# One table set for the roots, low weights a word past a line, constants behind the second piece

## The chip, the cores and the metric

The kernel runs on one core of one Trainium2 chip, as one program. The metric is the device time of an execution in microseconds, the median over several. A profiled execution adds the trace that the rows below are from; its span runs from the first to the last instruction.

## The reference

Two stages over 256 tokens of width 2048, all in fp32, and a final normalization. `first_block` has two layers, the first with an RWKV7 and RG-LRU mixer, the second with an attention over selected keys; `second_block` has two layers of three attentions side by side. What matters here:

```python
def rms_norm(x, g, eps=1e-6):
    xf = x.astype(jnp.float32)
    return (xf * lax.rsqrt(jnp.mean(xf * xf, -1, keepdims=True) + eps) * g).astype(x.dtype)

def layer_norm(x, g, b, eps=LN_EPS):
    ...
    return ((xf - mu) * lax.rsqrt(var + eps) * g + b).astype(x.dtype)

for layer in range(DEPTH):            # first_block
    y = ... @ w_out                   # the mixer, itself products of x
    x = layer_norm(DN_ALPHA * x + y, ...)
    x = layer_norm(DN_ALPHA * x + conv_ffn(x, ffn_w_up, ..., ffn_w_down), ...)
    x = x + sigmoid(x @ ple_w_gate) * (p @ ple_w_proj)
```

Nearly all of the work is products of the 2048 x 256 activations with weight matrices that are read once from memory.

## The kernel before

Activations are kept transposed, features on the 128 partitions and the 256 tokens in the free dimension, so a tensor of 2048 features is 16 tiles of 256 columns. A weight matrix comes in pieces of 128 x 4096 words (16 input tiles by 256 output features, 2,048 KB), which the SP queue brings into a ring of three slots (`load` and `stream`, L671 and L692). The second product of the feed-forward block has pieces of 11 input tiles (1,408 KB).

A product of fp32 numbers is made of three products of rounded ones (fp32r). ACT copies one half of a piece (128 output features, 128 x 2048 words) with rounding into the high weights `WHI` (`split`, L1771), and DVE subtracts these from the piece and writes the low weights `WLO` (`split`, by the helper at L2506). The activations have a high and a low part as well, side by side (`pair`). For each half, `wide_half` on PE runs 16 matmuls of the high weights on the 512 columns of both parts (L863), then 16 of the low weights on the 256 columns of the high part (L849). The feed-forward block's second product does the same with 11 and 11 (L968 and L973, weights `DHI` and `DLO`). A matmul is two instructions, a load of 128 columns of weights and the pass of the activations. PE waits on `w_hi` ahead of the high run and on `w_lo` ahead of the low one.

`spl_r` is a part of one big arena and holds high 0, low 0, high 1, low 1, each of 2048 words without a gap; `dsp_r` likewise with 1408 words each. All of them begin on a multiple of 32 bytes. `LG` and `BF` are other uses of the same words at other times.

An inverse root, 1/sqrt(v), is made on ACT as exp(-0.5 ln v). There are 16 places: the four layer norms in `normed` (L1896 and L1898), the norm of the keys in the first mixer (L2097 and L2099), two in `inverse_root` (L2235 and L2237), three in `rms` (L2332 and L2334), two `mn` (L2357 to L2360) and four `dn` (L2454 and L2456) in `second_block`. ACT holds one set of function tables at a time. The compiler puts an ACT_TABLE_LOAD right ahead of an ACTIVATE whose function the current set hasn't, and it takes one set for Ln and another for Exp, where one set would hold both. The Tanh of `second_block` (L2391) has no load of its own in the trace.

SP's queue begins with quarters of x and of the first piece ea0 in turn (`first_quarters`), then the second piece ea1, then `constants` (vec 789.5 KB, mat 896 KB, relb 2 KB, posi 129 KB; L654 to L657), then the third piece ea2, and from there each piece waits for its slot. DVE's first use of vec is the small set-up operation that writes `omm`.

Of the kernel before, what the change touches and what calls it, by code (L numbers as in the profile page):

```python
# [14 lines left out]
T = 256  # L15
P = 128
D = 2048
DT = D // P
# [6 lines left out]
SPL = 19456  # L25
# [2 lines left out]
MB = 5  # L28
FC = 11
HHW = FT * T  # L30
SCR = 2 * (HHW + FC * 2 * P) - 2 * T
PI_BELOW = 3.1415925
BIG_NEG = -1e30
NOT_ALLOWED = -3.0e38
# [190 lines left out]
def build(nc, dram, out):  # L225
# [38 lines left out]
    with ctx:  # L264
# [20 lines left out]
        FR = mybir.dt.float32r  # L285
        arena = nc.sbuf_base + (-nc.sbuf_base) % 32
        sb("arena", 2 * DT * T + SCR + 2 * T)
        X = DT * T

        def named(name, at_, width, dt=F):  # L290
            return nc.alloc_sbuf_tensor_at(name, [P, width], dt, offset=arena + 4 * at_)

        xa, xb, scr = named("xa", 0, X), named("xb", X, X), named("scr", 2 * X, SCR)
        xa_r, xb_r = named("xa_r", 0, X, FR), named("xb_r", X, X, FR)
        scr_r, spl_r = named("scr_r", 2 * X, 2 * HHW, FR), named("spl_r", 2 * X + SPL, 8192, FR)

        dsp_r = named("dsp_r", 2 * X + 2 * HHW, 4 * FC * P, FR)

        rstd = named("rstd", 2 * X + SCR, 2 * T)
        all_r = named("all_r", 0, 2 * X + SCR, FR)  # L300
        scrv = scr_r[:, :].rearrange("p (a t) -> p a t", t=T)
        allv = all_r[:, :].rearrange("p (a t) -> p a t", t=T)
        xav = xa[:, :].rearrange("p (a t) -> p a t", t=T)
# [6 lines left out]
        def v(name, i=0, n=1):  # L310
            return vec[:, VCOL[name] + i:VCOL[name] + i + n]
# [23 lines left out]
        S = {n: ctx.enter_context(nc.semaphore(n)) for n in names}  # L335
        x_part = [ctx.enter_context(nc.semaphore(f"x_part{i}")) for i in range(4)]
        w_part = [ctx.enter_context(nc.semaphore(f"w_part{i}")) for i in range(3)]
        w_ready = [ctx.enter_context(nc.semaphore(f"w_ready{i}")) for i in range(R3)]
# [19 lines left out]
        def job_free(j):  # L358
            return mb_free[j % MB]
# [47 lines left out]
        SE = sumbuf[:, 0:3 * T].rearrange("p (b t) -> p b t", t=T)  # L407
        KNB = sumbuf[:, 3 * T:5 * T]
        GNB = [sumbuf[:, (3 + n) * T:(4 + n) * T] for n in range(2)]
        LG = scr[:, SPL + 4096:SPL + 6144].rearrange("p (k n) -> p k n", n=P)  # L410
        VTOK = scr[:, 13056:15104].rearrange("p (t c) -> p t c", t=2)
        YT = tiles(15104, 16)
        XC = xbv[:, 0:8]
        KZ = xbv[:, 8:16]
        AR = xb[:, :].rearrange("p (a t x n) -> p a t x n", a=8, t=2, x=2)
        BF = [scr[:, SPL + 4096 * t:SPL + 4096 * t + 2048].rearrange("p (u x) -> p u x", u=16) for t in range(2)]
        GVB = [xtra[:, 1024 * t:1024 * (t + 1)].rearrange("p (u x) -> p u x", u=16) for t in range(2)]
        KF = [ring[:, SLOT + 512 * g:SLOT + 512 * (g + 1)].rearrange("p (u x) -> p u x", u=4) for g in range(4)]
        MN = [ring[:, SLOT + 512 * g:SLOT + 512 * (g + 1)].rearrange("p (u x n) -> p u x n", u=4, x=2) for g in range(4)]
# [76 lines left out]
        def squares(k):  # L496
# [11 lines left out]
        ANG = scr[:, 11776:12544]  # L508


        WHI, WLO = ([spl_r[:, 4096 * h + o:4096 * h + o + 2048].rearrange("p (k n) -> p k n", n=P)
                     for h in range(2)] for o in (0, 2048))

        DHI, DLO = ([dsp_r[:, FC * P * (2 * h + o):FC * P * (2 * h + o + 1)].rearrange("p (k n) -> p k n", n=P)
                     for h in range(2)] for o in range(2))
        HLO = scr_r[:, 0:HHW].rearrange("p (a t) -> p a t", t=T)


# [125 lines left out]
        def _(sp):  # L644
# [6 lines left out]
                        .then_inc(w_part[q] if q < 3 else w_ready[0], 16)  # L651

            def constants():
                sp.dma_start(vec[:, :], dram["vec"]).then_inc(S["in_vec"], 16)  # L654
                sp.dma_start(mat[:, :], dram["mat"]).then_inc(S["in_mat"], 16)
                sp.dma_start(relb[0:32, :], dram["relb"]).then_inc(S["in_mat"], 16)
                sp.dma_start(posi[:, :], dram["posi"]).then_inc(S["in_mat"], 16)  # L657
# [46 lines left out]
            load("ev_out", 0)  # L704

            sp.wait_ge(S["g_done"], STEP0["ev_out"] - 2)
            sp.dma_start(scr[:, SPL + 4096:SPL + 6144], dram["lg"][0]).then_inc(S["in_lg"], 16)

            sp.wait_ge(S["elem"], 3)
            for part in range(X_PARTS):  # L710
# [998 lines left out]
        def _(act):  # L1709
            A = nc.scalar.activation  # L1710
            count = [0]

            def unit_wait(name, k, i):

                act.wait_ge(S["g_done"], at(STEP0[name] + steps_of(name), k, i, steps_of(name)))
# [112 lines left out]
            def job_wait(key):  # L1828
                j = JOB[key]
                act.wait_ge(S["mb_done"], j + 1)  # L1830
                return job_bank(j)

            def normed(name, n, x, res):
# [16 lines left out]
                def embedded(k):  # L1850
                    u = UNIT0[f"pp{l}"] + k
                    act.wait_ge(S["g_done"], STEP0[f"pp{l}"] + k + 1)
                    A(PP[:, 2 * k + 6:2 * k + 8, :], unit_bank(u)[:, :].rearrange("p (a t) -> p a t", a=2), ACT.Copy)\
                        .then_inc(bank_free[u % R3], 2)
# [37 lines left out]
                if down_:  # L1892
                    split(nxt, 0, 0, 1, (0,))
                    embedded(0)
                act.wait_ge(S["ln_var"], n + 1)
                A(RV, RV, ACT.Ln, bias=v("eps")).then_inc(S["ln_log"], 1)  # L1896
                act.wait_ge(S["ln_log"], n + 1)
# [155 lines left out]
            for p in range(EV_HALVES + 1):  # L2053
# [40 lines left out]
                        A(KZ[:, i, :], ZK[:, i, :], ACT.Copy, scale=v("kk", i)).then_inc(S["kk_r"], 1)  # L2094
                if p == 31:
                    act.wait_ge(S["kk_sum"], 1)
                    A(KNB, KNB, ACT.Ln).then_inc(S["kk_log"], 1)  # L2097
                    act.wait_ge(S["kk_log"], 1)
                    A(KNB, KNB, ACT.Exp, scale=-0.5).then_inc(S["kk_rec"], 1)  # L2099
# [130 lines left out]
            def inverse_root(job, side, width):  # L2230

                b = job_wait((job, 0))
                key = JOB[(job, 0)]
                dst = rstd[:, side * T:(side + 1) * T]
                A(dst, b[:, 0:T], ACT.Ln, bias=v("eps_rms"), scale=1.0 / width).then_inc(job_free(key), 1)  # L2235
                act.wait_ge(job_free(key), freed(key))
                A(dst, dst, ACT.Exp, scale=-0.5).then_inc(S["c_q"], 1)  # L2237

            for p in range(8):
                k, half = p // 2, p % 2  # L2240
# [38 lines left out]
            for k in range(8):  # L2279
                u = UNIT0["uq"] + k  # L2280
# [23 lines left out]
            for t in range(16 + 3):  # L2304
                if 0 <= t - 2 < 16:
                    h = t - 2
                    b = job_wait(("PT", h))
# [10 lines left out]
                if 0 <= t - 3 < 16:  # L2318
                    h = t - 3
                    b = job_wait(("O", h))  # L2320
# [8 lines left out]

            def rms(n):  # L2330
                key = JOB[(f"rms{n}", 0)]
                A(RX, job_wait((f"rms{n}", 0))[:, 0:T], ACT.Ln, bias=v("eps_rms")).then_inc(job_free(key), 1)  # L2332
                act.wait_ge(job_free(key), freed(key))
                A(RX, RX, ACT.Exp, scale=-0.5).then_inc(S["h_std"], 1)  # L2334

            for l in range(2):
# [17 lines left out]
                pieces(name, 0, 4, later)  # L2354
                b = job_wait((f"mn{l}", 0))
                key = JOB[(f"mn{l}", 0)]
                A(rstd[:, 0:T], b[:, 0:T], ACT.Ln, bias=v("eps_rms"), scale=1.0 / 384)  # L2357
                A(rstd[:, T:2 * T], b[:, T:2 * T], ACT.Ln, bias=v("eps_rms"), scale=1.0 / 256).then_inc(job_free(key), 1)
                act.wait_ge(job_free(key), freed(key))
# [9 lines left out]
                for key, dst, n in ((f"mq{l}", QM, 3), (f"mk{l}", KN, 2)):  # L2369
                    for k in range(n):  # L2370
                        b = job_wait((key, k))
# [4 lines left out]
                for s in range(2):  # L2376
                    key = (f"mv{l}", s)
                    b = job_wait(key)
# [14 lines left out]
                for s in range(SLOTS):  # L2393
# [55 lines left out]
                    if s - 1 in DN_SLOTS:  # L2449
                        j = DN_SLOTS.index(s - 1)  # L2450
                        b = job_wait((f"dn{l}", j))
                        key = JOB[(f"dn{l}", j)]
                        rn = RN[:, 2 * j:2 * j + 2, :].rearrange("p a t -> p (a t)")
                        A(rn, b[:, :], ACT.Ln, bias=v("eps_rms"), scale=1.0 / 128).then_inc(job_free(key), 1)  # L2454
                        act.wait_ge(job_free(key), freed(key))
                        A(rn, rn, ACT.Exp, scale=-0.5).then_inc(S["d_q"], 1)  # L2456
# [1249 lines left out]
```

## Time and profile before

| | |
|---|---|
| median of 3 runs | 3287.39 us (3285.52 to 3289.57) |
| span of the profiled execution | 3284.6 us, 2.8 us below the median |
| PE busy | 3232.2 us (98%) |
| DVE busy | 2195.8 us (67%) |
| ACT busy | 1667.5 us (51%) |
| mean rate of the DMA | 172 GB/s |
| granted clock of PE | 9 tenths or more in each of 40 slices |

PE's busy time counts a matmul from its start to its modelled end, and in a dense run each starts before the one before has ended; the pace of a run is therefore read from the starts in the timeline. The profiled execution's own time is its span; the 2.8 us to the median are outside of it.

### The profile page before, as it was taken

The page shows a single profiled execution, that of the slowest core. Times are in us where ns is not written, and L with a number is a line of the kernel's source. Part 1 is how long each engine was busy: PE and PEld are TensorE (multiplying, and loading weights), DVE is VectorE, ACT ScalarE, POOL GpSimd, SP SyncE. Part 2 cuts the span into 40 slices and gives each one's busy share as a digit, 9 for nine tenths or more (in the row PEclk, how much of TensorE's full clock was granted, in tenths as well). Part 3 has the DMA queues.
Part 4 walks back from the last instruction along what each step waited for, and adds up shares of the span by engine and source line. Part 5 has one row for each costly group of instructions (what it writes and reads, how often), then busy time and mean ns, then how long its engine had stood idle before and what let it go on. Part 6 is the DMA issues. An engine that isn't in the chain of part 4 may idle for free.

```text
span 3284.6 us, 53186 instructions
## 1 busy us (share of the span) xinstructions
PE 3232.2 (98%) x21672; PEld 2855.1 (87%) x21672; DVE 2195.8 (67%) x2836; ACT 1667.5 (51%) x2138; POOL 24.5 (1%) x38
## 2 busy tenths in 40 slices
PE   9999999999999999999999999999999999999998
PEld 8888898888888888888888888888888888888887
DVE  6577767666676456676766666745675767647676
ACT  5574346555554335554555555533564456444563
POOL 0000000000000000011000000000000000000000
PEclk9999999999999999999999999999999999999999
DMA  7352145455444554534445445455544434444342
GB/s 279 143 210 67 57 167 200 181 188 196 179 185 175 184 190 183 190 119 180 164 181 199 182 186 198 159 186 192 188 168 185 171 129 167 186 175 167 129 171 112
DMA packets 47254, 563.64 MB, mean 172 GB/s; under 512 B 5072, under 2 KB 7264, under 8 KB 10720
## 3 DMA queue, kind: packets, MB, share of 16 engines
q1 hardware_dynamic: 47072, 561.06, 45.4%
q8 instruction: 133, 2.18, 0.3%
q14 instruction: 49, 0.40, 0.0%
HBM read 558.92 MB, written 2.12 MB: 171 GB/s over the span
## 4 chain that ended last, share of the span: by engine, by line
PE 90%; DVE 5%; ACT 3%; issue 2%; DMA 0%; SPq 0%; DVEq 0%; ACTq 0%
PE bank L863 40%; PE bank L849 21%; PE bank L968 10%; PE bank L973 5%; PE bank L1002 3%; ACT spl_r L1771 1%; PE bank L1468 1%; DVE ring L2506 1%; PE bank L784 1%; PE bank L788 1%; PE bank L782 1%; DVE spl_r L2506 1%; DVE xb L2506 1%; DVE xa L2506 0%; DVE scr L2506 0%
## 5 line engine op out<-in xcount | busy, mean ns | idle before, releaser
L2506 DVE TENSOR_TENSOR spl_r<-ring,spl_r 128x2048 fp32r<-128x2048 f32 (+2 forms) x429 | 961.3, 2242 | 485.8 <-ACT spl_r L1771 480.8
L863 PE MATMUL bank<-all_r,spl_r 128*128 128x512 f32 x4960 | 1196.6, 393 | 3.2 <-ACT spl_r L1771 3.2
L1771 ACT ACTIVATE spl_r<-ring 128x2048 fp32r<-128x2048 f32 x407 | 779.2, 1915 | 591.0 <-PE bank L849 484.1
L863 PEld LDWEIGHTS bank<-all_r,spl_r 128*128 128x128 f32 x4960 | 914.5, 188 | 189.5 <-issue 8.0
L849 PEld LDWEIGHTS bank<-all_r,spl_r 128*128 128x128 f32 x5008 | 642.1, 191 | 24.2
L849 PE MATMUL bank<-all_r,spl_r 128*128 128x256 f32 x5008 | 650.0, 283 | 0.0
L2506 DVE TENSOR_TENSOR dsp_r<-ring,dsp_r 128x1408 fp32r<-128x1408 f32 x126 | 204.8, 1625 | 206.4 <-ACT dsp_r L1771 206.2
L968 PE MATMUL bank<-scr_r,dsp_r 128*128 128x512 f32 x1386 | 338.8, 392 | 0.0
L1771 ACT ACTIVATE dsp_r<-ring 128x1408 fp32r<-128x1408 f32 x126 | 174.4, 1384 | 283.3 <-PE bank L973 283.1
L968 PEld LDWEIGHTS bank<-scr_r,dsp_r 128*128 128x128 f32 x1386 | 252.5, 189 | 47.4
L863 PE MATMUL bank<-scr_r,spl_r 128*128 128x512 f32 x1152 | 275.8, 391 | 2.9 <-ACT spl_r L1771 2.9
L863 PEld LDWEIGHTS bank<-scr_r,spl_r 128*128 128x128 f32 x1152 | 211.7, 188 | 45.0 <-issue 3.8
L2512 DVE SCALAR_TENSOR_TENSOR xtra<-sumbuf,vec,xtra 128x255 f32<-128x255 f32 (+1 forms) x352 | 170.2, 484 | 102.0 <-ACT xtra L1929 66.7
L973 PEld LDWEIGHTS bank<-scr_r,dsp_r 128*128 128x128 f32 x1386 | 182.9, 191 | 9.8
L1929 ACT ACTIVATE xtra<-sumbuf,vec 128x256 f32<-128x256 f32 x176 | 105.0, 598 | 168.1 <-DVE sumbuf L2506 168.1
L973 PE MATMUL bank<-scr_r,dsp_r 128*128 128x256 f32 x1386 | 185.9, 282 | 0.0
L849 PEld LDWEIGHTS bank<-scr_r,spl_r 128*128 128x128 f32 x1184 | 151.8, 191 | 5.6
L849 PE MATMUL bank<-scr_r,spl_r 128*128 128x256 f32 x1184 | 153.9, 283 | 0.0
L1935 ACT ACTIVATE xtra<-xtra 128x256 f32<-128x256 f32 x88 | 36.9, 419 | 160.5 <-DVE xtra L2512 160.5
L2506 DVE TENSOR_TENSOR sumbuf<-bank,sumbuf 128x256 f32<-128x256 f32 x275 | 114.7, 418 | 3.9 <-ACT sumbuf L1813 3.7
L1813 ACT ACTIVATE sumbuf<-bank 128x256 f32<-128x256 f32 x275 | 100.2, 365 | 15.6 <-PE bank L849 15.6
L2506 DVE TENSOR_TENSOR scr<-xtra 128x256 f32 (+1 forms) x88 | 37.5, 426 | 18.7 <-DVE xtra L2512 18.4
(437 smaller groups left out, 2673.9 us busy)
## 6 DMA issues: line engine op xcount, KB each, us to landing
ring<-in_up SPq DMA_DIRECT2D x88, 2048.0 KB, 7.8
ring<-in_down SPq DMA_DIRECT2D x64, 1408.0 KB, 6.0
ring<-in_ib SPq DMA_DIRECT2D x34, 2048.0 KB, 7.8
ring<-in_pg SPq DMA_DIRECT2D x16, 2048.0 KB, 7.8
ring<-in_out SPq DMA_DIRECT2D x16, 2048.0 KB, 7.9
ring<-in_in SPq DMA_DIRECT2D x12, 2048.0 KB, 7.7
ring<-in_ec SPq DMA_DIRECT2D x11, 2048.0 KB, 8.4
ring<-in_ea SPq DMA_DIRECT2D x8, 2048.0 KB, 10.5
```

The costliest lines, as they stand in the source:

```text
L782: mm(out_, WHI[half][:, kk, :], rhi[:, kk, :], start=kk == tile_order[0], stop=False)
L849: last_ = mm(main, WLO[half][:, kk, :], rhi[:, kk, :], start=False, stop=kk == DT - 1, skip_group_check=True)
L863: mm(b[:, :], WHI[half][:, kk, :], pair(name, kk), start=kk == 0, stop=False, skip_group_check=True)
L968: mm(b[:, :], high[:, kk, :], pair(name, piece * FC + kk), start=piece + kk == 0, stop=False, skip_group_check=True)
L973: one = mm(main, low[:, kk, :], HHI[:, high_slot(piece * FC + kk), :], start=False, stop=piece == 3 and kk == FC - 1, skip_group_check=True)
L1002: one = mm(out, lhsT, rhs, start=n == 0, stop=n == len(terms) - 1)
L1771: A(high[half], w[:, :, half * P:(half + 1) * P], ACT.Copy).then_inc(S["w_hi"], count)
L1813: A(dst, shape(sums(b, name)[1]), ACT.Copy).then_inc(S["low_act"], count)
L1929: one = A(GU[:, k % R3, half, :], SU[:, k % R3, half, :], ACT.Identity, bias=pick(v("cb", col, FT), index(k, i)), scale=pick(v("cw2", col, ...
L1935: A(GU[:, k % R3, 0, :], GU[:, k % R3, 0, :], ACT.Gelu_apprx_tanh).then_inc(S["up_gelu"], 1)
L2506: return V.tensor_tensor(out, a, b, op)
L2512: return V.scalar_tensor_tensor(out=out, in0=a, scalar=s, in1=b, op0=op0, op1=op1)
```

## The change

It has three parts, which have nothing to do with each other. Every root names the table set with both Ln and Exp ahead of its Ln (in `normed` ahead of the wait for the variance). The two low parts of the split weights begin one word past the boundary at which they began, in rooms that are eight words longer. The transfer of the constants, and with it all that SP issues after them, waits until the second piece has landed.

```diff
+HALF = 2048 + 8
+DOWN_HALF = FC * P + 8
+LOW_BEGIN = 1
+ROOM = 32
-SCR = 2 * (HHW + FC * 2 * P) - 2 * T
+SCR = 2 * (HHW + FC * 2 * P) - 2 * T + ROOM
...
-        scr_r, spl_r = named("scr_r", 2 * X, 2 * HHW, FR), named("spl_r", 2 * X + SPL, 8192, FR)
-
-        dsp_r = named("dsp_r", 2 * X + 2 * HHW, 4 * FC * P, FR)
+        scr_r, spl_r = named("scr_r", 2 * X, 2 * HHW, FR), named("spl_r", 2 * X + SPL, 4 * HALF, FR)
+
+        dsp_r = named("dsp_r", 2 * X + 2 * HHW, 4 * DOWN_HALF, FR)
...
-        all_r = named("all_r", 0, 2 * X + SCR, FR)
+        all_r = named("all_r", 0, 2 * X + SCR - ROOM, FR)
...
-        LG = scr[:, SPL + 4096:SPL + 6144].rearrange("p (k n) -> p k n", n=P)
+        LG = scr[:, SPL + 2 * HALF:SPL + 2 * HALF + 2048].rearrange("p (k n) -> p k n", n=P)
...
-        BF = [scr[:, SPL + 4096 * t:SPL + 4096 * t + 2048].rearrange("p (u x) -> p u x", u=16) for t in range(2)]
+        BF = [scr[:, SPL + 2 * HALF * t:SPL + 2 * HALF * t + 2048].rearrange("p (u x) -> p u x", u=16) for t in range(2)]
...
-        WHI, WLO = ([spl_r[:, 4096 * h + o:4096 * h + o + 2048].rearrange("p (k n) -> p k n", n=P)
-                     for h in range(2)] for o in (0, 2048))
-
-        DHI, DLO = ([dsp_r[:, FC * P * (2 * h + o):FC * P * (2 * h + o + 1)].rearrange("p (k n) -> p k n", n=P)
-                     for h in range(2)] for o in range(2))
+        def rounded_halves(tensor, room, n_tiles, low):
+
+            begins = [room * (2 * h + low) + LOW_BEGIN * low for h in range(2)]
+            return [tensor[:, b:b + n_tiles * P].rearrange("p (k n) -> p k n", n=P) for b in begins]
+
+        WHI, WLO = (rounded_halves(spl_r, HALF, DT, low) for low in range(2))
+
+        DHI, DLO = (rounded_halves(dsp_r, DOWN_HALF, FC, low) for low in range(2))
...
             def constants():
+                sp.wait_ge(w_ready[1], 16)
                 sp.dma_start(vec[:, :], dram["vec"]).then_inc(S["in_vec"], 16)
...
+            def roots():
+
+                nc.scalar.preload_act_table_set("natural_log_exp_and_others")
+
...
+                roots()
                 act.wait_ge(S["ln_var"], n + 1)
                 A(RV, RV, ACT.Ln, bias=v("eps")).then_inc(S["ln_log"], 1)
...
                 key = JOB[(f"rms{n}", 0)]
+                roots()
                 A(RX, job_wait((f"rms{n}", 0))[:, 0:T], ACT.Ln, bias=v("eps_rms")).then_inc(job_free(key), 1)
```

The call of `roots()` stands in the same way ahead of the Ln of the keys' norm, of `inverse_root`, of `mn` and of `dn`. The transfer into `LG` follows its new place.

## Rows read from the trace of the kernel before

**Rows 1.** The page: span and the busy time of each engine, with its instructions.

```profile
span 3284.6 us, 53186 instructions
...
PE 3232.2 (98%) x21672; PEld 2855.1 (87%) x21672; DVE 2195.8 (67%) x2836; ACT 1667.5 (51%) x2138; POOL 24.5 (1%) x38
```

**Rows 2.** The page: the chain that ended last, by line, share of the span.

```profile
PE bank L863 40%; PE bank L849 21%; PE bank L968 10%; PE bank L973 5%; PE bank L1002 3%; ACT spl_r L1771 1%; PE bank L1468 1%; DVE ring L2506 1%; PE bank L784 1%; PE bank L788 1%; PE bank L782 1%; DVE spl_r L2506 1%; DVE xb L2506 1%; DVE xa L2506 0%; DVE scr L2506 0%
```

**Rows 3.** PE's groups by form: count | busy, mean ns | idle before.

```profile
L849 PE MATMUL bank<-all_r,spl_r 128*128 128x256 f32 x5008 | 650.0, 283 | 0.0
...
L973 PE MATMUL bank<-scr_r,dsp_r 128*128 128x256 f32 x1386 | 185.9, 282 | 0.0
L849 PE MATMUL bank<-scr_r,spl_r 128*128 128x256 f32 x1184 | 153.9, 283 | 0.0
```

**Rows 4.** Timeline of PE, steady stretch: start us, duration us, instruction.

```profile
3158.29 3.82 PE L863 MATMUL bank<-all_r,spl_r 128*128 128x512 f32 x16
3161.95 2.08 PE L849 MATMUL bank<-all_r,spl_r 128*128 128x256 f32 x16
3163.86 3.82 PE L863 MATMUL bank<-all_r,spl_r 128*128 128x512 f32 x16
```

**Rows 5.** Narrow timelines of that stretch, and its window (busy us of each engine).

```profile
3159.45 2.66 PE L863 MATMUL bank<-all_r,spl_r 128*128 128x512 f32 x11
...
3162.06 0.40 PE L849 MATMUL bank<-all_r,spl_r 128*128 128x256 f32 x2
...
3158.29:3163.86 5.57, 5.57 (x34) 4.92 (x33) 4.12 (x6) 5.26 (x5) 0.00 (x0) 1.00 0.00 0
```

**Rows 6.** DVE's groups by form, shifted and unshifted operands.

```profile
L2512 DVE SCALAR_TENSOR_TENSOR xtra<-sumbuf,vec,xtra 128x255 f32<-128x255 f32 x176 | 85.2, 484 | 78.5 <-ACT xtra L1929 66.7 <-DVE xtra L2512 2.3
...
L2512 DVE SCALAR_TENSOR_TENSOR all_r<-xa,vec,all_r 128x256 fp32r<-128x256 f32 x32 | 14.1, 482 | 6.5 <-ACT xtra L1745 6.1
```

**Rows 7.** ACT's table loads by line: count | busy us, mean ns.

```profile
L1896 ACT ACT_TABLE_LOAD x4 | 5.1, 1283 | 0.1
...
L2368 ACT ACT_TABLE_LOAD x1 | 1.3, 1283 | 0.0
```

**Rows 8.** Timeline of the end, ACT and DVE.

```profile
3274.64 1.28 ACT L2334 ACT_TABLE_LOAD   x1
3275.93 0.42 ACT L2334 ACTIVATE vec<-vec 128x256 f32<-128x256 f32 x1
3276.38 4.63 DVE L2506 TENSOR_TENSOR xb<-xb,vec 128x1024 f32<-128x1024 f32 x4 [2.90 <-ACT vec L2334]
```

**Rows 9.** Timelines around the second layer norm, DVE and PE.

```profile
1251.57 2.29 DVE L2506 TENSOR_TENSOR spl_r<-ring,spl_r 128x2048 fp32r<-128x2048 f32 x1
...
1253.78 1.29 DVE L2506 TENSOR_TENSOR xa<-xb,xtra 128x512 f32<-128x512 f32 x2
...
1266.45 1.22 PE L885 MATMUL bank<-scr_r,spl_r 128*128 128x256 f32 x8 [0.70 <-ACT scr_r L1872]
```

**Rows 10.** Timelines of the start: first issue, pieces, set-up, PE.

```profile
0.75 0.38 SPq L649 DMA_DIRECT2D xa<-in_x  x1
...
19.32 1.91 ACT L1771 ACTIVATE spl_r<-ring 128x2048 fp32r<-128x2048 f32 x1 [3.75 <-DMA ring<-in_ea]
...
26.34 0.17 DVE L2509 TENSOR_SCALAR omm<-vec 128x27 f32<-128x27 f32 x1
...
29.53 1.92 ACT L1771 ACTIVATE spl_r<-ring 128x2048 fp32r<-128x2048 f32 x1 [2.08 <-DMA ring<-in_ea]
...
32.60 3.82 PE L863 MATMUL bank<-all_r,spl_r 128*128 128x512 f32 x16
```

**Rows 11.** Windows of the start: the last two columns are DMA share and GB/s.

```profile
0.00:19.30 19.30, 17.66 (x80) 14.72 (x80) 9.99 (x13) 10.16 (x13) 0.21 (x4) 1.00 0.91 351
19.30:29.50 10.20, 8.13 (x43) 7.08 (x44) 6.94 (x10) 4.97 (x6) 0.00 (x0) 1.00 1.03 425
1.00:2.00 1.00, 0.57 (x1) 0.50 (x2) 0.27 (x1) 1.00 (x1) 0.00 (x0) 1.00 0.25 37
```

More of the change, by code:

```diff
@@ L706, in _ @@
             sp.wait_ge(S["g_done"], STEP0["ev_out"] - 2)
-            sp.dma_start(scr[:, SPL + 4096:SPL + 6144], dram["lg"][0]).then_inc(S["in_lg"], 16)
+            sp.dma_start(scr[:, SPL + 2 * HALF:SPL + 2 * HALF + 2048], dram["lg"][0]).then_inc(S["in_lg"], 16)
             sp.wait_ge(S["elem"], 3)
@@ L2234, in inverse_root @@
                 dst = rstd[:, side * T:(side + 1) * T]
+                roots()
                 A(dst, b[:, 0:T], ACT.Ln, bias=v("eps_rms"), scale=1.0 / width).then_inc(job_free(key), 1)
@@ L2331, in rms @@
                 key = JOB[(f"rms{n}", 0)]
+                roots()
                 A(RX, job_wait((f"rms{n}", 0))[:, 0:T], ACT.Ln, bias=v("eps_rms")).then_inc(job_free(key), 1)
@@ L2356, in _ @@
                 key = JOB[(f"mn{l}", 0)]
+                roots()
                 A(rstd[:, 0:T], b[:, 0:T], ACT.Ln, bias=v("eps_rms"), scale=1.0 / 384)
@@ L2453, in _ @@
                         rn = RN[:, 2 * j:2 * j + 2, :].rearrange("p a t -> p (a t)")
+                        roots()
                         A(rn, b[:, :], ACT.Ln, bias=v("eps_rms"), scale=1.0 / 128).then_inc(job_free(key), 1)
```

## The prediction

> **What bounds the kernel now.** I read the page first, from the top. The reader is to see that TensorE (PE) is busy for 3232.2 of 3284.6 us while VectorE (DVE) has 67% and ScalarE (ACT) 51% [rows 1], and that the chain that ended last spends 40 + 21 + 10 + 5 = 76% of the span in L863, L849, L968 and L973, the two kinds of matmul of the weight streams [rows 2]. So a microsecond taken from ACT or DVE is worth nothing by itself; what counts is the pace of PE's matmuls and the few places at which PE waits, which are 52 us altogether (3284.6 - 3232.2).
>
> Next I read the groups of PE by form, for the numbers of matmuls. Those with low weights are 5008 + 1386 + 1184 = 7,578 [rows 3]; those with high weights are about as many. Durations in such groups overlap (a mean of 283 ns, though the next matmul starts far sooner), so the pace has to come from starts. PE's timeline in a steady stretch gives it: 16 matmuls of high weights on 512 columns take 3161.95 - 3158.29 = 3.66 us, and 16 of low weights on 256 columns take 3163.86 - 3161.95 = 1.91 us [rows 4]. Two narrower looks split these. The last eleven high ones take 3161.95 - 3159.45 = 2.50 us, 227.3 ns each, so the first five take 1.16 us, 232 each. The second low one starts at 3162.06, 0.11 us after the first; the other 15 take 3163.86 - 3162.06 = 1.80 us, 120.0 ns each [rows 5].
>
> Now the argument on which everything hangs. If a matmul took the time of its columns, 256 would take half of what 512 take: 227.3 / 2 = 113.6 ns, and the first interval of a low run (0.11 us) is such a one. The following ones take 120.0. Their columns can't be what they wait for; what is left is the load of the 128 columns of weights ahead of each, which has 227 ns to hide in in a high run and only 114 in a low one. The excess is 6.4 ns, over 7,578 matmuls 48.5 us. That is the largest sum in this kernel that a change of the place of the low weights can touch, and each nanosecond per low matmul is worth 7.6 us.
>
> **Part one: low weights a word past a line.** Nothing is added to any engine: same instructions, shapes and numbers. Three costs have to be priced.
>
> DVE writes the low weights in a place that is no longer aligned. What a shift costs DVE shows in the token shift: 128x255 elements read from one word on take 484 ns, an aligned 128x256 operation of the same kind 482 [rows 6], so nothing. If it cost something, the cover is this: DVE has one split of 2.29 us [rows 9] per 5.57 us of PE (3.66 + 1.91), and is busy for 4.12 of those 5.57 us [rows 5]; so it has 1.45 us per half piece before PE's low run would be late. The gelu and root operations behind it are no nearer to PE. The moved tensors (the LG and BF regions, the shortened all_r) change addresses alone: 0.
>
> PE reads the low weights unaligned. No row of the trace shows a weight load that doesn't begin on a line, so I bound it. From below: the load no longer stalls at all, the interval falls from 120.0 to 113.6, -48.5 us. It can't fall further, since then the columns set the pace. From above: a row of 128 words shifted by one touches one more line. A load of 128 columns at 120.0 ns is 0.94 ns a column; if the extra line costs as much as one or two columns, that is 0.94 x 7,578 = +7.1, or +14.2 us. Zero lies between and is a real candidate: an engine that reads word after word doesn't care where it begins. Which value? What could make a shift help is a stall between the load and the columns streaming past, both of which today start on the same kind of boundary; a stall that depends on how the two stand to each other. For that there is one row: in the first five matmuls of each high run, where loads stand otherwise to the columns, the excess over 227.3 is 232 - 227.3 = 4.7 ns instead of 6.4. So another phase costs 1.7 ns less; I take it as the nearest row to "the same loads in another phase": 1.7 x 7,578 = -12.9 us. It is a weak row, and the ends -48.5 and +14.2 stay for the range.
>
> A rule of the Trainium skill speaks against this part: "SBUF — State Buffer", in the note on cachelines, has 16-byte lines with a penalty for each cross to a new line, by which a shifted row of 128 words touches 33 lines instead of 32 and is slower. By it alone 120.0 x 33/32 adds 3.75 ns, an estimate of +28 us, where the row on the high run's first five gives -12.9.
>
> **Part two: one table set.** Today each of 16 root sites loads a table ahead of Ln and again ahead of Exp, 32 of 45 loads, 1.283 us each [rows 7] (the first and the last of 23 groups). After it there is one ahead of each root, and Ln and Exp share it. Tanh, which in second_block runs between the roots, has no load of its own today, so it shares Exp's present set. No row shows whether it is in the joint one; I take the worse case, a reload after each of the four dn roots and one more: 45 - 32 + 16 + 5 = 34 loads. ACT becomes about 14 us less busy (11 x 1.283), which at 51% is worth nothing where PE doesn't wait. Places where it does:
> - The end. In the last rms the load ahead of Exp starts at 3274.64 and Exp at 3275.93; DVE waits 2.90 us in all for the pair, and the output is behind it [rows 8]. The second load goes: -1.28 us. The first stays (its place is behind the squares either way).
> - The layer norms. After a down product Exp would end 1.28 us earlier, but DVE is in a split of 2.29 us from 1251.57 on, and what scales with the root starts at 1253.78, as that split ends. ACT's copies move up and PE's first wait shrinks, and PE waits again at 1266.45 for the last parts (0.70 us) [rows 9], whose pace DVE sets. I take 0 for both; the bound is -1.28 each, -2.6.
> - The other 13 sites: no wait of PE follows an Exp there. 0.
>
> Sum -1.3, bounds -3.9 and, if a reload lands in a waiting chain, +1.3. The Trainium skill, "ScalarE: Activation LUTs", section "What ACT_TABLE_LOAD costs", adds a drain of about 1.38 us to each load of 1.283. Here the Exp starts at 3275.93, within 0.01 us of its load's end, so the trace shows no drain; with it the end would give -2.66.
>
> **Part three: constants behind the second piece.** SP issues the second piece ea1, the four constants and ea2 one right behind the other in the first 8 us. The pieces are ready at 19.32 and 29.53 (ACT starts on them at once, after idling for the DMA) [rows 10]. What is queued behind the new wait on SP's queue: 4 constants (789.5 + 896 + 2 + 129 KB = 1.82 MB), ea2, then ea3, which waits for a free slot anyway. Until 19.3 the queue moves 351 GB/s: 6.77 MB, of which x, ea0 and ea1 are three times 2,048 KB = 6.29. So 0.49 MB of constants went along; these 0.49 MB now move after 19.3, at 425 GB/s 1.2 us. And the queue runs dry between ea1's arrival and the first bytes of vec: in the second from 1.00 to 2.00 only 37 GB/s flow after a first issue at 0.75 [rows 10, 11], so 1.0 to 1.5 us. Together 2.2 to 2.7 us; ea2 is ready at 29.53 + 2.4 = 31.9. ACT's split of its first half takes 1.92, so 33.9, and PE wants it at 32.60 [rows 10]: +1.3 us, less whatever ea1 gains by sharing with nobody (0 to 1.2, which also starts PE's second piece earlier). Bounds: -0.5 (ea1 earlier by what it shared, ea2 just in time) and +2.5. DVE's set-up ops, next to need vec and mat, run at 26.34 now [rows 10] and the constants land at about 19.3 + 1.25 + 1.82 MB / 425 GB/s = 24.8 to 26.4: just in time, and DVE has 4 us of idle around there. Late next would be the lows evicted through DVE, already in the bound.
>
> **Sum.** Profiled span 3284.6, and the median is 3287.4, 2.8 us above it, which I leave as it is. 3287.4 - 12.9 - 1.3 + 1.3 = 3274.5.
>
> **The rivals.** A measurement of this kernel can tell about 0.2%, 6.6 us, from no change: 0.87 ns per low load.
> - *The shift does nothing* (a rival on the claim itself). The 6.4 ns would be the bare length of a load of 128 columns, whatever its address. For: the excess stays through 15 intervals on end, like a fixed length. Against: the high run's first five, with a smaller excess. The loads of tables and the constants cancel: 3287.4, and up to 3290 with the upper bounds (+2.5).
> - *The shift costs* (slower). Place: the load ahead of each low matmul; price 0.94 ns per extra column's time, so 3294.5 for one, 3301.6 for two. It decides from 0.87 ns per load on. For: the load is the bound there, so any length added to it shows at once, in full. Against: nothing shows that a load is counted by lines. The skill's rule above is this rival.
> - *The full gain*: the interval falls to 113.6, 3287.4 - 48.5 = 3238.9, inside my forecast's own range. For: the excess is then all a clash. Against: one row says 4.7 of 6.4 remains.
> - *The tables move instead of going*: a reload directly behind each root. It would cost only the 1.3 at the end, 3275.8 with the forecast.
> - *The constants' wait in full*: +2.5 instead of +1.3, 3275.7.
>
> **Chances and range.** The shift helps by 0.87 ns per load or more: 0.42, forecast 3274.5, own range 3238 to 3280. It does nothing measurable: 0.36. It costs: 0.22. The last two small rivals move nothing across a bound. So faster 0.42, same 0.36, slower 0.22. The range has to hold both signs: from 3238 (the full gain; nothing lies below) to 3300 (between one and two extra columns), which leaves out the part of the slower case beyond it, some 0.1, and little else.
>
> **What would show it.** In the steady stretch, 16 low matmuls in less than 1.91 us (1.88 for the forecast, 1.82 for the full gain, 1.93 or more for the slower case), while the high run stays at 3.66. Table loads 34 instead of 45. At the end Exp directly behind Ln, and DVE's wait 2.90 down to 1.6. At 32.6 us PE waits for ACT, and ACT for the DMA of ea2, for about 1.3 us. The layer norm's last wait near 1266 unchanged. The prediction is wrong if the low run moves by more than 0.1 us up, if the high run changes with it, or if PE's waits elsewhere change by over 3 us.

## The result: 9 us slower, in the matmuls of the high weights

| | median | lowest to highest | runs |
|---|---|---|---|
| before | 3286.81 us | 3285.28 to 3289.57 | 8 |
| changed | 3295.70 us | 3293.92 to 3297.01 | 8 |

The ratio is 1.0028, with a 95% interval of 1.0019 to 1.0037. The forecast was 3274.5 us and faster; the time is inside the range of 3238 to 3300, on its other side. Beside the experiments below the kernel before was timed 84 times more; one of these executions took 12786 us and is left out of the ratios.

The head of the page of the changed kernel, which answers to [rows 1]:

```profile
span 3295.1 us, 53175 instructions
...
PE 3246.2 (99%) x21672; PEld 2854.3 (87%) x21672; DVE 2195.3 (67%) x2836; ACT 1653.1 (50%) x2127; POOL 24.5 (1%) x38
```

The span is 10.5 us longer and PE's busy time 14.0 (3246.2 - 3232.2), so PE idles 3.5 us less than before (48.9 against 52.4) and works more slowly. ACT's busy time fell by 14.4 us, to no effect. The timeline of PE in a steady stretch, which answers to [rows 4]:

```profile
3169.53 3.80 PE L871 MATMUL bank<-all_r,spl_r 128*128 128x512 f32 x16
3173.17 2.07 PE L857 MATMUL bank<-all_r,spl_r 128*128 128x256 f32 x16
3175.08 3.89 PE L871 MATMUL bank<-all_r,spl_r 128*128 128x512 f32 x16
3178.80 2.08 PE L857 MATMUL bank<-all_r,spl_r 128*128 128x256 f32 x16
3180.72 1.53 PE L871 MATMUL bank<-all_r,spl_r 128*128 128x512 f32 x6
```

L871 is L863 of before and L857 is L849. From start to start the high runs take 3.64 and 3.72 us, the low ones 1.91 and 1.92. Before it was 3.66 and 1.91 for every half piece. So the low runs, the place of the whole forecast, have not moved, and the high runs, which were to stay at 3.66, have split into two kinds in turn. Two half pieces take 3180.72 - 3169.53 = 11.19 us instead of 2 x 5.57 = 11.14. There are (5008 + 1184) / 16 = 387 half pieces of 16 tiles, 193 pairs: 0.05 x 193 = 9.7 us, the size of the result. The down product, whose half pieces of 11 tiles are not in this count, tells the same:

```profile
1010.65 2.67 PE L976 MATMUL bank<-scr_r,dsp_r 128*128 128x512 f32 x11
1013.15 1.47 PE L981 MATMUL bank<-scr_r,dsp_r 128*128 128x256 f32 x11
1014.46 2.73 PE L976 MATMUL bank<-scr_r,dsp_r 128*128 128x512 f32 x11
1017.03 1.47 PE L981 MATMUL bank<-scr_r,dsp_r 128*128 128x256 f32 x11
```

Its high runs take 2.50 and 2.57 us in turn, where those of before take 2.52. Two half pieces take 0.02 us more, over 63 pairs 1.3 us.

Two narrower looks at the steady stretch show how the two kinds differ, each with the last twelve matmuls of a high run:

```profile
3170.45 2.88 PE L871 MATMUL bank<-all_r,spl_r 128*128 128x512 f32 x12
3176.01 2.96 PE L871 MATMUL bank<-all_r,spl_r 128*128 128x512 f32 x12
```

The twelve of the first kind last until 3173.17, 2.72 us or 227 ns each, the pace that the prediction read for the last eleven of before. The twelve of the second last until 3178.80, 2.79 us or 232.5 ns each: this kind never gets down to 227.

The table loads, which answer to [rows 7], and the end, which answers to [rows 8]:

```profile
L1723 ACT ACT_TABLE_LOAD x16 | 20.5, 1283 | 0.8 <-DVEq L2789 0.5
L2408 ACT ACT_TABLE_LOAD x5 | 6.4, 1283 | 0.1
```

```profile
3284.68 1.28 ACT L1723 ACT_TABLE_LOAD   x1
...
3285.97 0.48 ACT L2348 ACTIVATE vec<-bank,vec 128x256 f32<-128x256 f32 x1
3286.48 0.42 ACT L2350 ACTIVATE vec<-vec 128x256 f32<-128x256 f32 x1
3286.93 4.63 DVE L2524 TENSOR_TENSOR xb<-xb,vec 128x1024 f32<-128x1024 f32 x4 [1.62 <-ACT vec L2350]
```

16 named loads, five reloads for Tanh, and 13 others: 34. DVE's last wait is 1.62 us instead of 2.90. The start, from the timeline, answers to [rows 10]:

```profile
19.14 1.91 ACT L1783 ACTIVATE spl_r<-ring 128x2048 fp32r<-128x2048 f32 x1 [3.73 <-DMA ring<-in_ea]
...
27.80 0.18 DVE L2527 TENSOR_SCALAR omm<-vec 128x27 f32<-128x27 f32 x1 [1.56 <-DMA posi<-in_posi]
...
32.43 1.91 ACT L1783 ACTIVATE spl_r<-ring 128x2048 fp32r<-128x2048 f32 x1 [3.51 <-DMA ring<-in_ea]
...
34.48 5.49 PE L871 MATMUL bank<-all_r,spl_r 128*128 128x512 f32 x16 [1.83 <-ACT spl_r L1783]
```

The third piece is ready at 32.43 (forecast 31.9), and PE waits 1.83 us for it, where it had waited for nothing. Windows around that wait (the last three columns are the granted clock as a share of full speed, the DMA's share and GB/s):

```profile
32.60:34.50 1.90, 0.07 (x2) 0.05 (x1) 0.13 (x1) 1.90 (x2) 0.00 (x0) 1.00 1.09 466
34.50:35.50 1.00, 1.00 (x3) 0.86 (x4) 1.00 (x1) 0.98 (x2) 0.00 (x0) 0.64 0.89 377
35.50:36.50 1.00, 1.00 (x4) 0.71 (x4) 1.00 (x1) 0.99 (x3) 0.00 (x0) 0.50 1.15 492
```

Behind the wait the clock falls to 0.50, the lower of its two levels, 1.2 GHz, and the high run that starts at 34.48 needs 5.3 us until the low one begins, against 3.75 for the one at 21.19, which stands behind a wait of 1.82 us and no fall of the clock.

### The profile page after: what moved, and what is told of

Same layout as the page of the kernel before. It is cut to its first block, busy times and chain, and to the rows that moved or that the text cites. A ratio compares the mean times of both kernels' runs of the same rounds, so it can differ in the third digit from the quotient of the medians.

```text
span 3295.1 us, 53175 instructions
## 1 busy us (share of the span) xinstructions
PE 3246.2 (99%) x21672; PEld 2854.3 (87%) x21672; DVE 2195.3 (67%) x2836; ACT 1653.1 (50%) x2127; POOL 24.5 (1%) x38
## 4 chain that ended last, share of the span: by engine, by line
PE 90%; DVE 5%; ACT 3%; issue 1%; DMA 1%; SPq 0%; DVEq 0%; ACTq 0%
PE bank L871 41%; PE bank L857 21%; PE bank L976 10%; PE bank L981 5%; PE bank L1010 3%; ACT spl_r L1783 1%; PE bank L1476 1%; DMA ring<-in_ea 1%; DVE spl_r L2524 1%; DVE xb L2524 1%; PE bank L796 1%; PE bank L792 1%; PE bank L790 1%; DVE xa L2524 1%; PE bank L1299 1%
## 5 line engine op out<-in xcount | busy, mean ns | idle before, releaser
L871 PE MATMUL bank<-all_r,spl_r 128*128 128x512 f32 x4960 | 1207.4, 396 | 4.4 <-ACT spl_r L1783 4.4
L871 PEld LDWEIGHTS bank<-all_r,spl_r 128*128 128x128 f32 x4960 | 914.5, 188 | 199.1 <-issue 9.6
L857 PEld LDWEIGHTS bank<-all_r,spl_r 128*128 128x128 f32 x5008 | 640.8, 188 | 25.9
L857 PE MATMUL bank<-all_r,spl_r 128*128 128x256 f32 x5008 | 649.3, 281 | 0.0
L871 PE MATMUL bank<-scr_r,spl_r 128*128 128x512 f32 x1152 | 277.9, 393 | 2.9 <-ACT spl_r L1783 2.9
L871 PEld LDWEIGHTS bank<-scr_r,spl_r 128*128 128x128 f32 x1152 | 211.4, 188 | 46.7 <-issue 3.6
L857 PEld LDWEIGHTS bank<-scr_r,spl_r 128*128 128x128 f32 x1184 | 151.5, 188 | 6.0
L857 PE MATMUL bank<-scr_r,spl_r 128*128 128x256 f32 x1184 | 153.7, 281 | 0.0
```

What stands on the lines that cost most here:

```text
L857: last_ = mm(main, WLO[half][:, kk, :], rhi[:, kk, :], start=False, stop=kk == DT - 1, skip_group_check=True)
L871: mm(b[:, :], WHI[half][:, kk, :], pair(name, kk), start=kk == 0, stop=False, skip_group_check=True)
```

## The experiments

Each was timed in five rounds beside the kernel before on the same chip. They fall in four groups on three chips, in which the medians of before are 3287.44, 3286.93, 3286.64 and 3287.18 us, so medians of different groups can be compared to about 1 us. The three parts come first, each alone on the kernel before; then the places of the weights, with neither of the other two parts. Each layout is told by how many bytes past a multiple of 128 from the begin of the split weights the four halves stand (high 0, low 0, high 1, low 1). Before all four are at 0. The changed kernel has 0, 36, 64, 100: its rooms of 2056 words also move the second high half, by 16 words. Where the whole arena stands is known only to 32 bytes, and it is the same in all.

| kernel | bytes past 128 | high runs, us | low runs, us | median, us | ratio, interval |
|---|---|---|---|---|---|
| before | 0, 0, 0, 0 | 3.65, 3.66 | 1.91 | 3287 | 1 |
| table set alone | as before | 3.65, 3.66 | 1.91 | 3286.14 | 0.9998, 0.9989 to 1.0007 |
| places alone | 0, 36, 64, 100 | 3.63 and 3.73 | 1.91, 1.92 | 3295.75 | 1.0028, 1.0017 to 1.0038 |
| constants alone | as before | 3.65, 3.66 | 1.91 | 3289.07 | 1.0006, 0.9997 to 1.0015 |
| rooms, no word | 0, 32, 64, 96 | 3.66 and 3.72 | 1.89, 1.88 | 3288.98 | 1.0007, 0.9998 to 1.0016 |
| low at 32 | 0, 32, 0, 32 | 3.68 | 1.89 | 3282.70 | 0.9986, 0.9977 to 0.9995 |
| low at 36 | 0, 36, 0, 36 | 3.67 | 1.91, 1.90 | 3291.32 | 1.0012, 1.0003 to 1.0021 |
| low at 4 | 0, 4, 0, 4 | 3.66 | 1.88, 1.89 | 3281.82 | 0.9983, 0.9974 to 0.9992 |
| low at 64 | 0, 64, 0, 64 | 3.66 | 1.88 | 3275.15 | 0.9960, 0.9946 to 0.9974 |
| high 1 apart | 0, 64, 64, 64 | 3.67 and 3.74 | 1.88, 1.89 | 3293.13 | 1.0020, 1.0011 to 1.0029 |
| low apart | 0, 32, 0, 96 | 3.66, 3.67 | 1.89, 1.88 | 3277.08 | 0.9972, 0.9962 to 0.9983 |
| low at 96 | 0, 96, 0, 96 | 3.66 | 1.88, 1.87 | 3271.19 | 0.9953, 0.9940 to 0.9967 |
| both high at 64 | 64, 32, 64, 32 | 3.73 | 1.91 | 3317.11 | 1.0090, 1.0076 to 1.0104 |

The runs' lengths are from start to start in a stretch near 1840 us of each trace, to 0.01 us.

**The table set alone.** The edit is the diff of `roots()` and its calls, nothing else.

> The table set part alone. The theory from the two traces: the end gains 1.3 us, each of the two layer norms behind a down product gains 1.2 us at the matmuls of L986 and gives some 0.7 back at the last parts, the two others about 0.9 together; in all 3 to 4 us less than before, ratio 0.9990. Rival, my prediction's own sum: 1.3 us less. Rival two: part of the waits that differ came from the shifted start, and this run shows none of them but the end. The pace of the weight products (16 high in 3.65 us, 16 low in 1.91) is as before.

Measured: 0.9998, no difference that the measurement can tell; the theory's 0.9990 lies just inside the interval as well. The trace speaks against it. PE's waits at L986, in all 2.1 us before, are gone, as expected. What the norm gives there it takes back further on; the timeline of PE at the last layer norm, of this kernel:

```profile
2349.82 7.09 PE L986 MATMUL bank<-xtra,ring 128*128 128x256 f32 x32
...
2361.51 1.21 PE L897 MATMUL bank<-scr_r,spl_r 128*128 128x256 f32 x8 [0.39 <-DVE scr_r L2516]
...
2365.04 1.21 PE L897 MATMUL bank<-scr_r,spl_r 128*128 128x256 f32 x8 [0.41 <-DVE scr_r L2516]
...
2367.11 1.22 PE L885 MATMUL bank<-scr_r,spl_r 128*128 128x256 f32 x8 [0.85 <-ACT scr_r L1876]
...
2369.66 0.75 PE L885 MATMUL bank<-scr_r,spl_r 128*128 128x256 f32 x4 [0.37 <-ACT scr_r L1876]
...
2373.99 3.89 PE L863 MATMUL bank<-scr_r,spl_r 128*128 128x512 f32 x16 [0.24 <-ACT spl_r L1775]
```

From the start of these matmuls of L986 to the next weight stream it is 2373.99 - 2349.82 = 24.17 us. The timeline of before at the same place, and its window behind the norm's first wait:

```profile
2347.62 5.34 PE L986 MATMUL bank<-xtra,ring 128*128 128x256 f32 x24
...
2371.79 3.91 PE L863 MATMUL bank<-scr_r,spl_r 128*128 128x512 f32 x16 [0.24 <-ACT spl_r L1771]
```

```profile
2358.00:2363.00 5.00, 4.93 (x29) 4.96 (x30) 4.97 (x6) 4.31 (x8) 0.00 (x0) 0.66 0.97 406
```

It is 24.17 us here too, so this norm gives nothing. The waits of the kernel with the table set, 0.39 + 0.41 + 0.85 + 0.37 = 2.0 us, are not in the trace of before at this norm, but that is in part the clock: in its profiled execution the clock fell there (0.66 in the window) and PE was too slow to wait. The kernel with low weights at 64, with the tables of before and the full clock at this norm, waits 0.72 + 0.39 us for the last parts and takes 24.16 us. So PE arrives earlier and waits for the same parts, and slow matmuls ahead of such a wait cost nothing. What stays in the trace is the end's 1.28 us.

**The places alone.** The edit is the diff of `HALF`, `DOWN_HALF`, `LOW_BEGIN`, `ROOM` and of all that uses them.

> The new places of the split weights alone (rooms of 8 words more, and the one word). Theory: the whole loss of pace seen in the changed kernel is here: high runs of 3.64 us and of 3.73 us in turn instead of 3.65, low runs of 1.91, about 12 us more than before (ratio 1.0037). Rival: the clock drop at the start or the moved waits set the runs out of step, then this run has 3.65 us throughout and ratio 1.000.

Measured: 1.0028, the ratio of the whole change, with the two kinds of high run. The rival, that the start sets the runs out of step, is out.

**The constants alone.**

```diff
             def constants():
+                sp.wait_ge(w_ready[1], 16)
```

> The wait of the constants alone. Theory: PE waits 1.9 us at about 32.6 us for the third piece, the granted clock falls to half for some 3.6 us behind it, another 1.6 us; together 3.5 us late at 40 us, of which 1.6 us comes back at about 144 us where PE waits for ACT in any case: 1.9 us more than before, ratio 1.0006. Rival: nothing comes back, ratio 1.0011. My prediction had 1.3 us.

Measured: 1.0006, 1.6 us by the medians (3289.07 against 3287.44), within what the measurement can't tell from zero. Its trace is not the one expected. Timeline of the start:

```profile
21.35 5.50 PE L864 MATMUL bank<-all_r,spl_r 128*128 128x512 f32 x16 [2.25 <-ACT spl_r L1772]
...
32.58 1.92 ACT L1772 ACTIVATE spl_r<-ring 128x2048 fp32r<-128x2048 f32 x1 [3.50 <-DMA ring<-in_ea]
...
34.64 3.90 PE L864 MATMUL bank<-all_r,spl_r 128*128 128x512 f32 x16 [0.33 <-ACT spl_r L1772]
```

Here the clock fell behind the earlier wait, at 21.35, which every version has (2.29 us before). That made PE late by some 1.6 us, and so the wait for the third piece was only 0.33 us. Its windows say the same:

```profile
22.00:23.00 1.00, 1.00 (x4) 0.81 (x3) 1.00 (x1) 1.00 (x1) 0.00 (x0) 0.50 1.03 427
23.00:24.00 1.00, 1.00 (x3) 0.75 (x3) 1.00 (x3) 0.55 (x2) 0.00 (x0) 0.50 1.01 422
```

The kernel with the table set alone, whose start is that of before, has the same drop at 22 to 26 us, and of the 16 traces in all eight have it. So the drop there comes with the execution and not with the constants.

**Rooms without the word.**

```diff
-LOW_BEGIN = 1
+LOW_BEGIN = 0
```

> The places of the changed kernel without the one word: low weights begin on the boundary, but the rooms are 8 words longer, so that high 1 begins 16 words later against high 0 than before. Theory: the 3.64 and 3.73 us in turn come from the two high halves standing differently, so they are here too, with low runs of 1.91 us: 10 to 12 us more than before (1.0035). Rival: it is the one word that breaks the step of the loads, then the high run is 3.65 us throughout here and the time is that of before (1.000).

Measured: 1.0007, not clear of no change, where the theory had 1.0035. The two kinds of high run are here, so the word does not make them. But the low runs got shorter, which I had not expected, and this pays for the high ones. Timeline:

```profile
1839.83 2.05 PE L856 MATMUL bank<-all_r,spl_r 128*128 128x256 f32 x16
1841.72 3.89 PE L870 MATMUL bank<-all_r,spl_r 128*128 128x512 f32 x16
1845.44 2.04 PE L856 MATMUL bank<-all_r,spl_r 128*128 128x256 f32 x16
1847.32 3.83 PE L870 MATMUL bank<-all_r,spl_r 128*128 128x512 f32 x16
1850.98 1.23 PE L856 MATMUL bank<-all_r,spl_r 128*128 128x256 f32 x9
```

Low 1.89 and 1.88, high 3.72 and 3.66. The word on top of it costs 3295.75 - 3288.98 = 6.8 us: it takes the low runs back to 1.91.

**High halves in step, four places of the low ones.** The second half of the weights begins 4160 words after the first (a multiple of 128 bytes, for the down weights 2880), and the low weights `LOW_BEGIN` words behind the end of the high ones: 8, 9, 1 and 16.

```diff
-HALF = 2048 + 8
-DOWN_HALF = FC * P + 8
-LOW_BEGIN = 1
-ROOM = 32
+HALF = 2048 + 32
+DOWN_HALF = FC * P + 32
+LOW_BEGIN = 8
+ROOM = 128
...
-            begins = [room * (2 * h + low) + LOW_BEGIN * low for h in range(2)]
+            begins = [2 * room * h + (n_tiles * P + LOW_BEGIN) * low for h in range(2)]
```

> Both high halves begin on a multiple of 128 bytes as in the kernel before, the low ones 32 bytes past such a multiple, no odd word. Theory (the slow high runs come from the second high half standing 64 bytes off the first): high runs of at most 3.66 us throughout, low runs between 1.88 and 1.89 as with the rooms alone, so about 28 ns less per half piece, 13 us less than before, ratio 0.996. Rival (where the low weights stand decides how the high run goes): high runs of 3.72 us in half of the cases again and a ratio of 1.000 to 1.003.

> As the run before it, with the one word more: low weights 36 bytes past a multiple of 128. Theory: the high runs are 3.64 us throughout, as they were in every second half of the changed kernel, low runs 1.906: 24 ns less per half piece, 11 us less, ratio 0.9966. Rival: high runs of 3.73 in half or all of the cases, 8 to 30 us more.

> Low weights one word past a multiple of 128 bytes, high ones on it: the one word by itself, with no room in between that shifts anything. My prediction's likeliest case would show here at its purest: low runs under 1.91 us and high runs at 3.65, ratio 0.996. Theory: the single word changes the low run by less than 1% and leaves the high run within 0.02 us, ratio 0.998 to 1.001. The slower rival of the prediction: low runs of 1.93 us or more.

> Low weights 64 bytes past a multiple of 128, high ones on it. Theory (a load and the columns that pass clash by place within 128 bytes): low runs differ from both 1.91 and 1.88, high runs of at most 3.66. Rival: only a multiple of 64 bytes or not matters, then low runs are 1.91 us and the ratio is 1.000.

In all four the high runs are of one kind, so the second kind has gone with the second half's 64 bytes. My sizes for the first two were wrong: 3.68 and 3.67 us are longer than 3.66, so that a low half at 32 leaves only 4.2 us of its gain, and one at 36 loses 4.4. So where the low weights stand also moves the high run a little, by 0.02 us. The one word alone, at 4, gains 5.1 us, a ratio within the theory's, though its low run got 1.5% shorter and not under 1%; 64 gains 11.8. The low runs of these two are alike. What parts them are the high runs, above all those of the down product, which the table leaves out: 2.55 us at 4 and 2.52 at 64 as before, 3.8 us over 126 half pieces. Timeline of the kernel at 64:

```profile
1839.56 3.82 PE L870 MATMUL bank<-all_r,spl_r 128*128 128x512 f32 x16
1843.22 2.05 PE L856 MATMUL bank<-all_r,spl_r 128*128 128x256 f32 x16
1845.10 3.82 PE L870 MATMUL bank<-all_r,spl_r 128*128 128x512 f32 x16
```

High 3.66, low 1.88: each low matmul is faster by some 0.03 / 16 = 1.9 ns, and the high runs are as before. Over all undisturbed low runs of the two traces the commonest length is 1.913 us before and 1.886 here, which is 1.7 ns per matmul.

**The second high half, or the low ones.** The first kernel is the one at 64 with high 1 moved by 64 bytes, as counted past a multiple of 128 (in words high 1 begins 48 earlier and low 1 32 earlier than there); the second has the low halves of the rooms' layout and the high ones in step.

```diff
+            begins = [2 * n_tiles * P * h + (16 if h and not low else 0) + low * (n_tiles * P + 16 + 32 * h) for h in range(2)]
...
+            begins = [2 * room * h + low * (n_tiles * P + 8 + 16 * h) for h in range(2)]
```

> The best layout so far (low weights 64 bytes past a multiple of 128 from the begin of the split weights) with one thing moved: the second high half stands 64 bytes off the first, as in the changed kernel. Theory: this alone makes high runs of 3.72 us and of 3.65 us in turn, 8 to 17 us more than the best layout, 3283 to 3292 us. Rival: the places of the low halves against each other made the two kinds, then both high runs are 3.65 and the time is 3275.

> Both high halves in step, the low ones 32 and 96 bytes past a multiple of 128, as the rooms of the changed kernel set them, without the word. Theory: no high run over 3.69 us, time near 3283 us as with both at 32. Rival: high runs of 3.72 in turn, as in the run with the rooms alone, 3289 us; then the low halves are the cause.

High 1 alone costs 3293.13 - 3275.15 = 18.0 us, 1 more than I had expected at most. The lows apart do not make the second kind: 3277.08, better than the 3283 foreseen. Timeline of the first:

```profile
1840.63 3.90 PE L870 MATMUL bank<-all_r,spl_r 128*128 128x512 f32 x16
1844.37 2.05 PE L856 MATMUL bank<-all_r,spl_r 128*128 128x256 f32 x16
1846.25 3.83 PE L870 MATMUL bank<-all_r,spl_r 128*128 128x512 f32 x16
1849.92 2.05 PE L856 MATMUL bank<-all_r,spl_r 128*128 128x256 f32 x16
```

High runs of 3.74 and 3.67 in turn, with low runs that both stay short.

**At 96, and both high halves at 64.** The first has `LOW_BEGIN = 24`. The second moves all by 16 words more:

```diff
+            begins = [2 * room * h + 16 + low * (n_tiles * P + 24) for h in range(2)]
```

> Low weights 96 bytes past a multiple of 128, high ones on it, the one class of 32 bytes not yet seen. Theory (only the place against the high weights counts, and 96 is to 0 as 0 is to 32): low runs of 1.89, high runs between 3.65 and 3.69, 3275 to 3283 us. Rival: low runs of 1.91 as at 0, then 3287 us.

> Both high halves stand 64 bytes further on, in step with each other, and both low ones 96 bytes past their high ones, as in the run with 96. It tells whether the slow high run comes from the second half standing elsewhere than the first, or from standing elsewhere than the activations that pass. Theory (against the activations): every high run is 3.73 us now, some 36 us more than the run with 96, 3307 us. Rival (against each other): high runs of 3.66 us and 3272 us.

At 96 the time is 3271.19 us, better than the 3275 to 3283 foreseen. With both high halves 64 bytes on it is 3317.11, 10 more than the theory's 3307, and the timeline has one kind of high run, the slow one:

```profile
1839.78 3.89 PE L870 MATMUL bank<-all_r,spl_r 128*128 128x512 f32 x16
1843.51 2.07 PE L856 MATMUL bank<-all_r,spl_r 128*128 128x256 f32 x16
1845.42 3.89 PE L870 MATMUL bank<-all_r,spl_r 128*128 128x512 f32 x16
1849.15 2.07 PE L856 MATMUL bank<-all_r,spl_r 128*128 128x256 f32 x16
```

Both high runs take 3.73 us. So a half is not slow because it stands elsewhere than the other half, but because of where it stands itself: at 64 it was slow in four layouts, with its low half at 32, 64, 96 and 100, at 0 never. The theory had left out the low runs. At 1.91 us against 1.88 at 96 they make about 12 us by the lengths in the two traces, beside some 29 of the high runs and 8 of the down product, a little more together than the 46 between the medians. The low halves are at 32 here, where with the high ones at 0 the low run took 1.89; so the place past a multiple of 128 does not settle the low run's pace alone. Nor does the weights' place settle all: in the same trace the streams of 28 to 49 us, with other activations, have high runs of 3.75 and low ones of 1.92. The activations were never moved, and high halves only stood at 0 and 64. Whether the place counts against the activations or against the memory as such, and whether 128 bytes is the right measure, is open.

**The table set on the two best layouts.**

> The best layout and the one table set together, without the constants' wait. Theory: the sum of the two alone, 11.7 + 0.7 us less than before: 3274 us, ratio 0.9958, and at the end DVE waits 1.6 us instead of 2.9. Rival: PE being faster, its waits at the layer norms grow and the roots are worth 3 to 4 us there: 3271 us.

> The layout with the low weights at 96, and the one table set. Theory: the gains add, 3271.2 less 1 to 2 us, 3270 us, ratio 0.995; Exp directly behind Ln at the end. Rival: the granted clock's drop at the start hides the difference, 3271 to 3273 us.

With the low weights at 64 and the table set: 3273.07 us, ratio 0.9958 (0.9944 to 0.9971), where the layout alone had 0.9960. At 96 with it: 3272.82, ratio 0.9953 (0.9940 to 0.9967), the ratio of the layout alone. The traces show the 1.3 us of the table set at the end; no time here tells them from zero. By the ratios either kernel is 23 to 25 us faster than the changed one (0.9958 and 0.9953 against 1.0028), and 14 to 15 faster than before.

## Why the prediction was wrong, step by step

**The bound** was read rightly: PE's pace decides, and 14 us less of ACT bought nothing that the times show. That the shift costs DVE nothing was right as well: its busy time is 2195.3 us, where it was 2195.8.

**Low weights a word past a line, -12.9 us: this step failed.** It measured +8.3 by the medians, +9 by the ratio (places alone, 1.0028). It failed in two ways. First, "Nothing is added to any engine: same instructions, shapes and numbers" passed over what the rooms do: eight words after each half put the second high half 16 words further on. I had priced the moved tensors at "change addresses alone: 0" while arguing in the next paragraph that an address can change a matmul's pace. Moving that half alone costs 18.0 us on the 64-byte layout. I had even written "while the high run stays at 3.66" as a sign, and it was this that broke. Second, the low runs did not gain, because the word stood on top of a move by 32 bytes or 96: the lows took 1.89 us at 32 bytes and 1.91 at 36, 1.88 at 96 and 1.92 at 100.

The idea behind the number holds, though: a part of the 6.4 ns depends on place. That it is a clash of loads and columns no run shows. The estimate of 1.7 ns less in another phase comes out as 1.7 at 64 bytes, and its 12.9 us as 11.8, but that is luck: the row said nothing on any place, and the places tried gave from 0.4 ns (36) to 2.2 (96). It was put on a layout that doesn't have it. Nor are the high run's slower first intervals a fixed phase: over the traces there are two of them in the changed kernel's faster kind, five before, nine with the lows at 32, and in the slower kind they go on to the end. The full gain of 48.5 us showed in no layout; the shortest low run was 1.87 us where 1.82 would have been needed.

**The slower rival** named the right sign and size (+7.1 to +14.2 us) by luck, with a wrong mechanism. It put the price on the load ahead of each low matmul, and in the changed kernel low runs are 1.91 as before. Its purest form, one word past a multiple of 128 bytes, is the run at 4: low runs of 1.88 and 1.89 us, 5.1 us less in all. The Trainium skill, "SBUF — State Buffer", in the note on cachelines, has a penalty for each cross to a new 16-byte line; an estimate by it was 3.75 ns more per load. The runs agree with it in two places and not in a third. By the commonest lengths, one word more, and so one line more per row, went with 0.9 ns more from 32 to 36 bytes and 2.4 from 96 to 100, but with 1.8 less from 0 to 4.

**The table set, -1.3 us.** Right in the trace, by steps too, and too small for the times: 34 loads, DVE's last wait from 2.90 to 1.62 us, no gain left at the layer norms, where the waits at L897 and L885 take it back. The bound of -3.9 was not reached. The Trainium skill, "ScalarE: Activation LUTs", section "What ACT_TABLE_LOAD costs", would add a drain of 1.38 us; Ln starts at 3285.97, 0.01 us after its load's end at 3284.68 + 1.28, and the wait fell by 1.28 us alone, so again none is seen.

**The constants, +1.3 us.** Within its bounds: the third piece came at 32.43 instead of 31.9, and alone it measured +1.6 to +2.0 us (1.0006), which is not clear of zero. The constants themselves landed later than the 24.8 to 26.4 of the prediction: DVE waited 1.56 us for them, until 27.80, and had the idle time for it. The step did not speak of the clock. In the changed kernel's trace the wait of 1.83 us was followed by 1.6 us more from slow matmuls; whether the new wait makes that more likely than the one at 21 us is not shown.

## What to carry to other kernels

An edit that makes room shifts what stands behind it. When a pace is suspected to depend on place, list where every operand of that engine stands, before and after, and not only the one that the edit is about. To try a place, move one operand at a time, by steps of 32 bytes and by the single word, and read the start-to-start times of one run of matmuls: 0.05 us in 11 decided this case. A median alone (1.0007) would have hidden that the rooms made the high runs longer and the low ones shorter. The same word cost 6.8 us on the rooms and 8.6 on the lows at 32 (3291.32 - 3282.70), and gained 5.1 on the layout of before. In a kernel that waits for several producers in turn, a wait removed on one comes back on the next, as at the layer norms.

## What the runs showed that I had not expected

The place of weights changes the pace of fp32r matmuls. With high weights at a multiple of 128 bytes from the begin of their tensor 16 matmuls on 512 columns took 3.63 to 3.68 us, and 64 bytes off 3.72 to 3.74. The low ones, on 256 columns, took 1.91 us at 0, 1.87 to 1.89 at 4, 32, 64 and 96, and 1.90 to 1.92 at 36 and 100; with the high ones at 64 bytes they took 1.91 at 32 as well. The kernel's time went from 3271 to 3317 us over layouts that differ in nothing else.

A wait of PE of 1.8 to 2.3 us within the first 35 us was followed by the lower clock (0.50) for some 3 to 4 us in some executions and not in others: behind the wait at 21 us in eight of the 16 traces, among them those of the table set alone and of the constants alone, and not in the profiled one of before. It costs 1.6 us there. Each trace has more such stretches further on, and one at a layer norm cost nothing, so how much of the spread between executions comes from the first is not shown.
